# Which engine adds the expert values of the last layer: one value in four moved from TensorE to VectorE

## What is computed

```python
def _peer(h, wq, sub_keys, u_tab, v_tab):
    ...
    idx = jnp.take_along_axis(cidx, pos, axis=-1)      # 8 heads x 16 experts per token
    g = jax.nn.softmax(top, axis=-1).astype(h.dtype)
    def block(args):
        x_i, i_i, g_i = args
        u = jnp.take(u_tab, i_i, axis=0)
        a = jax.nn.gelu(jnp.einsum('td,thkd->thk', x_i, u))
        return jnp.einsum('thk,thkd->td', a * g_i, jnp.take(v_tab, i_i, axis=0))
```

## Time and profile before

| | us |
|---|---|
| median of 3 runs | 5250.2 |
| lowest and highest run | 5249.68, 5269.2 |
| the profiled execution, its own time | 5245.18 |
| its span, first to last instruction | 5243.3 |

### The profile page before, as it was taken

The page is one execution under the profiler, slowest core; times in us unless marked ns, Lnnn a source line. Parts: engine busy times, 40 slices in busy tenths (PEclk is TensorE's granted clock), DMA queues, the critical chain, the costliest instruction groups (busy, mean ns, idle before and its releaser), DMA issues.

```text
span 5243.3 us, 38881 instructions
## 1 busy us (share of the span) xinstructions
PE 4137.8 (79%) x12290; PEld 2083.4 (40%) x12290; DVE 3290.9 (63%) x8016; ACT 791.4 (15%) x2180; POOL 1746.6 (33%) x1444
## 2 busy tenths in 40 slices
PE   8778988989888767677666799899877777677776
PEld 3565633454333333235332463345433323233232
DVE  0247876577876566665668588647776666755554
ACT  1212311100111111111111241100111111111111
POOL 0101244331233344443333224424124434334343
PEclk9889998999999888789887899899988888988898
DMA  6345665665799999999998576556469999999998
GB/s 239 129 176 191 241 227 203 237 228 192 311 395 387 363 378 388 391 375 389 388 386 314 192 250 225 205 208 249 163 251 381 364 386 364 366 395 399 379 394 322
DMA packets 221849, 1576.21 MB, mean 301 GB/s; under 512 B 26337, under 2 KB 28674, under 8 KB 31692
## 3 DMA queue, kind: packets, MB, share of 16 engines
q0 software_dynamic: 184320, 1342.26, 65.5%
q1 hardware_dynamic: 37324, 231.47, 11.6%
HBM read 1570.71 MB, written 2.92 MB: 300 GB/s over the span
## 4 chain that ended last, share of the span: by engine, by line
PE 41%; DMA 24%; DVE 20%; issue 5%; POOL 4%; ACT 3%; DVEq 0%; POOLq 0%; SPq 0%; ACTq 0%
PE ps L946 18%; DMA sb_arena<-in_peer_uv,sb_idx 11%; DMA sb_gbufs<-in_peer_uv,sb_idx 11%; PE ps L876 7%; DVE sb_gbufs L1545 4%; DVE sb_arena L1545 3%; PE ps L824 2%; PE ps L854 2%; PE ps L914 2%; DVE sb_eacc L1568 2%; POOL sb_gbufs L1749 1%; PE ps L644 1%; ACT sb_dge L1159 1%; PE ps L739 1%; PE ps L756 1%
## 5 line engine op out<-in xcount | busy, mean ns | idle before, releaser
L1749 POOL DMA_INDIRECT sb_gbufs<-in_peer_uv,sb_idx x768 | 948.4, 1235 | 1922.1 <-PE ps L946 930.1
L946 PE MATMUL ps<-sb_gbufs,sb_dge 128*128 128x512 f32 x1856 | 966.8, 679 | 364.6 <-ACT sb_dge L1159 364.6
L946 PE MATMUL ps<-sb_arena,sb_dge 128*128 128x512 f32 x1856 | 956.4, 673 | 368.3 <-ACT sb_dge L1159 368.3
L1545 DVE CUSTOM_DVE_ANT_0 sb_arena<-sb_arena,sb_keep 128x1024 f32<-128x1024 f32 x512 | 621.7, 1228 | 496.4 <-DMA sb_arena<-in_peer_uv,sb_idx 495.3
L1545 DVE CUSTOM_DVE_ANT_0 sb_gbufs<-sb_gbufs,sb_keep 128x1024 f32<-128x1024 f32 x512 | 622.4, 1228 | 482.1 <-DMA sb_gbufs<-in_peer_uv,sb_idx 480.6
L1749 POOL DMA_INDIRECT sb_arena<-in_peer_uv,sb_idx x512 | 578.2, 1129 | 953.8 <-PE ps L946 918.7
L946 PEld LDWEIGHTS ps<-sb_gbufs,sb_dge 128*128 128x128 f32 x1856 | 395.7, 219 | 904.1 <-issue 521.5
L946 PEld LDWEIGHTS ps<-sb_arena,sb_dge 128*128 128x128 f32 x1856 | 392.1, 217 | 898.0 <-issue 464.7
L1154 ACT ACTIVATE sb_small<-sb_small 128x4 f32<-128x4 f32 x256 | 52.6, 206 | 2476.1 <-DVE sb_small L1556 2476.1
L1568 DVE SCALAR_TENSOR_TENSOR sb_eacc<-sb_gbufs,sb_small,sb_eacc 128x1024 f32<-128x1024 f32 x299 | 405.1, 1355 | 9.0 <-DVE sb_small L1579 0.2
L1545 DVE CUSTOM_DVE_ANT_0 sb_gbufs<-sb_gbufs,sb_h2p 128x1024 f32<-128x1024 f32 x256 | 330.2, 1308 | 34.6 <-DMA sb_gbufs<-in_peer_uv,sb_idx 34.4
(11 more groups left out here) (218 smaller groups left out, 4119.1 us busy)
## 6 DMA issues: line engine op xcount, KB each, us to landing
sb_ring<-in_w_ada SPq DMA_DIRECT2D x48, 1024.0 KB, 7.9
sb_ring<-in_w_wq SPq DMA_DIRECT2D x32, 1024.0 KB, 7.3
sb_ring<-in_w_hy SPq DMA_DIRECT2D x24, 1024.0 KB, 8.0
sb_ring<-in_w_ga SPq DMA_DIRECT2D x16, 1024.0 KB, 7.2
sb_ring<-in_w_gb SPq DMA_DIRECT2D x16, 1024.0 KB, 8.7
sb_ring<-in_w_oab SPq DMA_DIRECT2D x16, 1024.0 KB, 8.0
sb_ring<-in_dft_s SPq DMA_DIRECT2D x16, 1024.0 KB, 8.4
sb_ring<-in_w_out SPq DMA_DIRECT2D x14, 1024.0 KB, 7.7
```

The lines of the kernel that those rows point to most:

```text
L946: q = pe.matmul(ps[:, c, :], dge[:, b, :], gbuf[b][:, D + c * 512:D + c * 512 + 512], start=(h == 0 and i == 0), stop=(h == HALVES - 1 and ...
L1545: dve.tensor_tensor_reduce(gbuf[b][:, 0:D], gbuf[b][:, 0:D], h2, 1.0, 0.0, ALU.mult, ALU.add, dots[:, q:q + 1]).then_inc(Z["ttr"], 1)
L1749: nc.gpsimd.indirect_dma_start(out=gbuf[b], out_offset=None, in_=I["peer_uv"], in_offset=bass.IndirectOffsetOnAxis(ap=idx[:, col:col + 1], ...
```

## The change

```diff
 def by_vector(layer, t):
-    return 1 if layer < DEPTH - 1 and t > 1 else 0
+    return 1 if t > 1 else 0
```

## The result

| | before | changed |
|---|---|---|
| median of 12 runs, us | 5251.15 | 5272.36 |
| lowest and highest | 5243.29, 5269.20 | 5264.71, 5283.68 |
| the profiled execution, us | 5245.18 | 5277.69 |
| its span, us | 5243.3 | 5275.9 |

The changed kernel takes 1.0036 times as long, with a 95% interval of 1.0025 to 1.0047. That is +19 us on 5251 by the ratio and +21 by the medians; the forecast was 5266, with 5238 to 5300 as its range. The difference is real, and under the 0.5% that the prediction set as its bound for "slower". The prediction held that a difference under 0.5% can't be told from none on this kernel; with 12 runs of each kernel, a third of a per cent could be.

A forecast was written before the change was run, and what follows sets the result against it. The prediction took a loop through TensorE and the DMA gathers, neither alone, to bound the kernel. Its terms 9.0 + 2.4 + 1.9 + 3 - 0.5 gave +15.8 us, forecast 5266 us on the median's footing, range 5238 to 5300.

The forecast's parts named there:

- the forecast case: Whole kernel: the summed terms give +15.8 us, forecast 5266 us; 5255 to 5285 was given a chance of 0.47.
- rival C: Routing pieces absorb the multiply-add, since shorter bursts give back VectorE's loss; 5250 to 5253 us, tile 2 not growing; chance 0.22.
- rival A: TensorE's share counts: each step gains if its last gather is what the loop waits for; -46 us, above 5220; chance 0.10.
- TensorE's 163 us priced at nothing: 96 shorter bursts save about 163 us of TensorE's busy time, nearly all worth nothing, as gather releases keep their distance.
- The steady step at nothing: VectorE's 1.285 us multiply-add delays the first dot about 0.9 us, the second and last start on time; price 0.
- the normalisations: Three normalisations at a tile's fourth step stand behind a multiply-add; half of 3 x 1.28 us, +1.9 us.
- The pieces of routing, +9.0: Tile 2: the multiply-add delays routing pieces on VectorE while the DMA is empty; seven of eight pay 1.28 us, +9.0 us.
- The clock, +3: Shorter bursts leave TensorE idle longer, so rows of short bursts, about two of 48 pairs, become impossible; +3 us.
- within 0.3: Tiles 3 and 4: the period of a pair of steps was to stay at 21.3 us within 0.3.
- Rival B: Bursts of twelve stay at the low clock to their third slot, in both groups; +43 us, 5306 us; chance 0.20.
- The tile ends and the tail, +2.4 and -0.5: Line 1612 ahead of the weights at two tile ends, +2.4 us; shorter last burst against line 1612 and its wait, -0.5 us.
- The rule on the DMA's duration: Gather estimated at 4.4 us, not 6.15, making the slower loop 11.1 us, under 12.4, and the clock term 0; rejected.

The follow-up runs named there:

- t_three_only: Changed kernel without VectorE's additions in layer 1, the fourth value left out of the output; 1.0014 of the kernel before, +6.5 us between the medians.
- v_adds_not_at_pieces: Kernel before plus a thrown-away VectorE multiply-add per step, tiles 2 to 4 of layer 1, except eight steps ahead of routing pieces; 1.0009 of the kernel before.
- v_adds_only: Kernel before plus a thrown-away VectorE multiply-add in every step of tiles 2 to 4 of layer 1; 1.0022 of the kernel before, +11.8 us between medians.

## Why the prediction was right, and where it was off

- **The direction and the time** (+16 forecast, +19 to +21 measured) came out, by the terms of the forecast case. Tile 2 grew by 9.4 us, as the sign against rival C had it. It was not a case of rival A: no tile became shorter. Taking the work from TensorE without giving it to VectorE cost 6.5 us (t_three_only).
- **TensorE's 163 us priced at nothing.** Right. The page shows 102 us less busy time, as the slower clock ate the rest, and none of it in the span.
- **The steady step at nothing.** Right as far as it is shown: the timeline has the first dot late by 0.8 us and the second on time. With 88 multiply-adds outside the pieces v_adds_not_at_pieces is at 1.0009 (0.9994 to 1.0024); 1.9 us of that were forecast for the normalisations, and a small price of the steady steps isn't excluded.
- **The pieces of routing, +9.0.** Right in place, and somewhat high: 7 and 6 us by the two pairs of timed runs, 10.4 and 4.2 in the profiled tile 2. All of VectorE's part was forecast at 9.0 + 1.9 without line 1612 and measured at 11.8, so what isn't at the pieces, some 5 us, was more than the 1.9; where it lies isn't shown.
- **The clock, +3.** This term was too small. Measured it is 6.5 us (0.0014, interval 0.0001 to 0.0027), most of it in tile 3. The step that failed is "more short bursts turning long in the other group cost nothing in this reckoning, since a pair pays for the slower loop once". The number of slow bursts went from 48 to 72 of 96 (the prediction counted 47 short ones, in a window that holds 94). Tile 3 went from 342.8 / 16 = 21.4 us a pair to 353.8 / 16 = 22.1, which fails the test "within 0.3" (not by the clock alone: v_adds_only, at a clock of 0.88, has 350.0 / 16 = 21.9); tile 4 went from 21.5 to 21.7 and passes it. That a pair pays only once was argued from single loops. What the runs show in its place: the first issue came late in both groups (the table of first issues), and in t_three_only, where no multiply-add moves the dots, the first dot of `gbufs` in tile 3 came on average 4.05 us after the dot before it instead of 3.74 and that of `arena` 2.69 instead of 2.57. That is 0.43 us a pair, or 7 us in the tile, which is its whole loss, and most of it lies in the group that was slow before. Why the slow group loses more when the other becomes slow isn't shown.
- **Rival B** had the low clock in both groups with a price of 43 us, and it came to a seventh of it: the slow bursts took 6.8 to 8.5 us, and most of them under 8.
- **The tile ends and the tail, +2.4 and -0.5.** Not separated. The rest behind the last tanh fell from 21.2 to 19.2 us, for the last burst happened to start at full clock: it took 5.42 us, not the 7.0 of the forecast. The lines that follow it are as foreseen:

```profile
5257.58 5.42 PE L946 MATMUL ps<-sb_arena,sb_dge 128*128 128x512 f32 x12 [1.46 <-ACT sb_dge L1159]
5263.03 1.22 DVE L1612 TENSOR_TENSOR sb_eacc<-ps,sb_eacc 128x1024 f32<-128x1024 f32 x1 [4.62 <-PE ps L946]
5264.29 1.23 DVE L1614 TENSOR_TENSOR sb_eacc<-sb_eacc,sb_g 128x1024 f32<-128x1024 f32 x1
5265.55 1.23 DVE L1618 TENSOR_TENSOR sb_x<-sb_x,sb_eacc 128x1024 f32<-128x1024 f32 x1
```

- **The rule on the DMA's duration** (the Trainium skill, DMA: Bandwidth & Descriptors, Anatomy of one DMA) would have made the clock free. It is not: the kernel before gains 1.3% when its bursts start at full clock. But the row that the prediction set against it was misread: at the issue at 4612.63 two gathers of `arena` were still under way (their dots start at 4613.82 and 4616.29), so 6.15 us is not the time of a gather with no queue. Behind the last piece of routing, with all buffers landed, the issue at 4550.43 had its dot 5.50 us later:

```profile
4555.93 1.23 DVE L1545 CUSTOM_DVE_ANT_0 sb_gbufs<-sb_gbufs,sb_keep 128x1024 f32<-128x1024 f32 x1 [4.67 <-DMA sb_gbufs<-in_peer_uv,sb_idx]
```

That is 1.1 us above the 4.4 us that the prediction estimated by the Trainium skill, and with it the slower loop would be 2.60 + 4.05 + 5.50 = 12.15 us, under 12.40. So the sum of the single loop doesn't explain the late gathers; that they come from the slow starts is shown by the filler alone.

## What to carry to other kernels

Where a transfer is released by an engine's burst, ask how soon after its start the burst releases the first buffer; here that counted, and not how long the burst lasted or how busy the engine was. Taking work from such an engine can then slow the kernel, and adding work that nobody needs behind the release can speed it up. Work put on an engine with idle time is free only where that time lies: ask which long pieces on that engine it stands ahead of, and charge up to its full length for each (here 6 to 7 us for eight of 1.28). And read the rate of a transfer queue, not its busy share.

## What was not expected of the hardware

- Six records of useless matmuls behind each burst raised the granted clock from 0.88 to 1.00 and the gather rate over 4600 to 5150 us from 391 GB/s to 416, and took 1.3% off the whole kernel (4 runs).
- The DMA share was 0.98 at 384 GB/s and 1.01 at 416 GB/s: over most of this stretch it can't tell a starved queue from a full one.
- With the multiply-adds alone on VectorE the clock stayed at 0.88, yet tile 3 took 350.0 us against 342.8, and 346.5 in v_adds_not_at_pieces, whose tile 3 runs the same instructions. So a tile's time in one execution scatters by 3 us and more, and differences of single tiles below that carry nothing.
